# A two-block transformer kernel on one core: in the second block's skewed norms, ScalarE writes each shifted tile one weight unit later

## The chip, the cores and the metric

The kernel runs on one core of a Trainium2 chip. The metric is the device time of one execution in microseconds. Five things work side by side in a core: TensorE multiplies (PE in the profile; PEld is its loading of the stationary operand), VectorE (DVE), ScalarE (ACT), GpSimd (POOL), and SyncE (SP), which here only issues DMAs. Each engine takes its own instructions strictly in order; they meet through semaphores, on which an engine stops until another has counted far enough.

## The reference

The program is two transformer blocks in a row, each of two layers, on 256 tokens of width 1024. The first block mixes windowed attention, a short convolution and blocked attention, then a SwiGLU. The second block has two streams of 256 tokens, context and latent. A stream goes through an adaptive norm, a SwiGLU with a gated residual, a mixer (convolution, latent attention, Fourier mixing) and another SwiGLU, all modulated by vectors from a conditioning input. What matters here is the norm before each part:

```python
def rms_norm(x, g):
    xf = x.astype(jnp.float32)
    y = xf * lax.rsqrt(jnp.mean(xf * xf, axis=-1, keepdims=True) + EPS)
    return (y * g.astype(jnp.float32)).astype(x.dtype)

def ada_norm(h, g, shift, scale):
    return rms_norm(h, g) * (1 + scale) + shift

# in second_block, for each layer
h = h + HALF * gt1 * swiglu_2(ada_norm(h, g_ffn1[l], sh1, sc1), w1_ffn1[l], w3_ffn1[l], w2_ffn1[l])
u = ada_norm(h, g_mix[l], sh2, sc2)
```

## The kernel before

**Units.** All weights stream once through the core in 850 units. A unit is 128 output features by up to 8 blocks of 128 inputs, 512 KB. Each unit passes four steps. SP loads it into one of four slots (`raw`). ACT rounds it to the multiplier's precision (`high`, the CAST at L606, `whi<-raw`). DVE makes the remainder (`low`, L1141, `wlo<-raw,whi`). PE multiplies: three products per block (high by high, high by low, low by high; L2042 to L2044, or L1960 to L1962 where two units are interleaved), so 24 matmuls of 256 columns for one stream of 256 tokens. ACT and DVE work three units ahead (`AHEAD = 3`). `high` of unit u waits until PE has finished unit u-4, whose slot it takes.

**Tiles of the activations.** They lie with features on the partitions, in eight tiles (`m` = 0 to 7) of 128 by 512 columns: the context stream in columns 0 to 255, the latent stream in 256 to 511. They are split into a high and a low part too (`uhi`, `ulo`).

**The skewed norm.** The norm of one stream is hidden behind the matmuls of the other. While PE goes through a stage of units for the other stream, ACT squares the residual's tiles (L754), POOL adds the squares (L534), PE sums over features, ACT takes the root (L759), DVE inverts it, and PE spreads it over the partitions. Then each tile takes three steps:

- DVE scales it, `half_apply` (L1478, `big<-h,scl,aux`);
- ACT adds the shift and rounds, `half_shift` (L765, `uhi<-big,mod`);
- DVE makes the remainder, `half_low` (L1484, `ulo<-big,mod,uhi`).

The tables `DOWN`, `UP`, `INTO`, `INTO_LAST` and `AT_CHANGE` say after which unit j of the stage each tile is taken: one or two tiles per unit. In ACT's and DVE's programs a function `then(j)` is called at the end of step j of the stage. A step of ACT is: `high` of unit j+3, what else ACT does for unit j (a bank read out, the square of a tile), then `then(j)`. A step of DVE is: what it does for unit j (in the down stages the residual update, L1666), `low` of unit j+3, then `then(j)`, which scales the tiles of j and makes the remainders of the tiles of j-1. So DVE makes a remainder one unit after it scaled that tile.

**Where it is used.** Nine passes over a stage carry such a norm: the context part of the second block's first down projection (`fdown100c`), the second pass of four down or output projections (`fdown102`, `bout0`, `fdown202`, `fdown112c`; called a seam, with the table `DOWN`), and the first units of the stage behind each of those four (`mix0`, `fup200c`, `fup110c`, `mix1`). One more such norm, of the context stream beside the first block's last stages, is ordered by a function of its own that the diff leaves alone.

**What follows.** The stage for which a norm was made begins with two units interleaved (`two_units`, L1960): PE first waits for the `low` of both, and then, block by block, for one tile's remainder each.

## Time and profile before

| | |
|---|---|
| median of 3 runs | 3005.26 us (3005.05 to 3005.29) |
| span of the profiled execution | 3003.9 us |
| PE busy | 2897.1 us, 96% |
| DVE busy | 2051.9 us, 68% |
| ACT busy | 1366.5 us, 45% |
| POOL busy | 153.3 us, 5% |
| chain that ended last | PE 82%, DVE 9%, ACT 4%, issue 3%, DMA 2% |

The profiled execution has no device time of its own in the profile beside its span; the median of the unprofiled runs is 1.4 us longer than that span. PE's matmuls overlap: each lasts some 0.28 us while the next starts 0.11 us after it. So a share of 96% can still hide short stops, and where a row says that PE was idle for x us, the starts lie x + 0.28 us apart instead of 0.11, so that about 0.17 us more than x is lost. Line numbers are those of the kernel before.

### The profile page before, as it was taken

What the parts mean: (1) busy time and instruction counts of PE and PEld (TensorE: products, weight loads), DVE (VectorE), ACT (ScalarE), POOL (GpSimd) and SP (SyncE); (2) the same over time, 40 slices, a digit from 0 to 9 for tenths busy, and PEclk for the clock granted to TensorE, in tenths of its full rate; (3) what the DMA queues carried; (4) which work ended last, traced back from release to release, by engine and by line L of the source; (5) the groups of instructions that cost most, each with busy time, mean ns of one, the idle gap of its engine ahead of it and who ended that gap; (6) DMA issues with size and microseconds to landing.
All of it is one profiled execution on the core that took longest, in us unless ns stands there. A gap on an engine that the chain in (4) does not pass through costs nothing.

```text
span 3003.9 us, 59994 instructions
## 1 busy us (share of the span) xinstructions
PE 2897.1 (96%) x23648; PEld 2789.5 (93%) x23648; DVE 2051.9 (68%) x3323; ACT 1366.5 (45%) x2212; POOL 153.3 (5%) x222
## 2 busy tenths in 40 slices
PE   8999999999999999999999999999999999899998
PEld 8889999888999999998889999999999999779998
DVE  4658786658678777778764476867768566876655
ACT  5555445555446432354544354223542235545543
POOL 0000000000000000010000020000200001000000
PEclk9999999999999999999999999999999999999999
DMA  6435764435666565552212354544645445225454
GB/s 235 146 115 187 243 235 163 149 108 176 211 210 198 193 222 194 177 184 67 81 45 89 105 185 161 206 156 171 208 162 207 144 152 187 64 82 192 161 184 138
DMA packets 148053, 487.54 MB, mean 162 GB/s; under 512 B 16400, under 2 KB 25872, under 8 KB 147728
## 3 DMA queue, kind: packets, MB, share of 16 engines
q1 hardware_dynamic: 126688, 407.22, 41.0%
q0 software_dynamic: 21168, 77.60, 7.6%
q8 instruction: 135, 2.21, 0.3%
q14 instruction: 62, 0.51, 0.1%
HBM read 482.66 MB, written 1.05 MB: 161 GB/s over the span
## 4 chain that ended last, share of the span: by engine, by line
PE 82%; DVE 9%; ACT 4%; issue 3%; DMA 2%; POOL 0%; DVEq 0%; ACTq 0%; SPq 0%; POOLq 0%
PE bank L2042 23%; PE bank L2043 22%; PE bank L2044 22%; DVE wlo L1141 3%; ACT whi L606 2%; PE bank L1960 2%; PE bank L1961 2%; PE bank L1962 2%; DVE acc L1742 2%; PE aux L2269 1%; PE bank L2287 1%; DMA bbb<-in_w_ada 1%; PE bank L2120 1%; DMA raw<-in_w_stream 1%; DMA big<-in_w_ada 1%
## 5 line engine op out<-in xcount | busy, mean ns | idle before, releaser
L2042 PE MATMUL bank<-uhi,whi 128*128 128x256 f32 x4968 | 1397.0, 281 | 9.6 <-DVE wlo L1141 6.0
L2044 PE MATMUL bank<-uhi,wlo 128*128 128x256 f32 x4968 | 1381.1, 278 | 0.0
L2043 PE MATMUL bank<-ulo,whi 128*128 128x256 f32 x4968 | 1380.9, 278 | 0.0
L1141 DVE TENSOR_TENSOR wlo<-raw,whi 128x1024 fp32r<-128x1024 f32 (+4 forms) x850 | 951.0, 1121 | 370.7 <-ACT whi L606 362.2
L2042 PEld LDWEIGHTS bank<-uhi,whi 128*128 128x128 f32 x4968 | 935.1, 188 | 28.2 <-issue 22.9
L606 ACT CAST whi<-raw 128x1024 fp32r<-128x1024 f32 (+4 forms) x850 | 811.5, 961 | 282.7 <-PE bank L2044 179.3
L2043 PEld LDWEIGHTS bank<-ulo,whi 128*128 128x128 f32 x4968 | 934.8, 188 | 3.4 <-issue 3.0
L2044 PEld LDWEIGHTS bank<-uhi,wlo 128*128 128x128 f32 x4968 | 937.7, 189 | 0.0
L2042 PE MATMUL bank<-yhi,whi 128*128 128x256 f32 x1740 | 494.1, 284 | 16.2 <-DVE wlo L1141 8.5
L2043 PE MATMUL bank<-ylo,whi 128*128 128x256 f32 x1764 | 491.3, 279 | 0.0
L2044 PE MATMUL bank<-yhi,wlo 128*128 128x256 f32 x1740 | 484.5, 278 | 0.0
L2042 PEld LDWEIGHTS bank<-yhi,whi 128*128 128x128 f32 x1740 | 328.9, 189 | 25.4 <-issue 10.1
L2043 PEld LDWEIGHTS bank<-ylo,whi 128*128 128x128 f32 x1764 | 333.3, 189 | 3.2 <-issue 2.7
L2044 PEld LDWEIGHTS bank<-yhi,wlo 128*128 128x128 f32 x1740 | 329.8, 190 | 0.0
L706 ACT CAST yhi<-pp 128x256 fp32r<-128x256 f32 (+3 forms) x108 | 53.8, 498 | 320.7 <-DVE pp L1328 320.5
L1328 DVE TENSOR_TENSOR pp<-pp,bank 128x256 f32<-128x256 f32 (+1 forms) x108 | 57.6, 533 | 201.1 <-PE bank L2044 201.1
L1216 DVE CUSTOM_DVE_ANT_0 acc<-big,cs 128x1024 f32<-128x1024 f32 x128 | 156.3, 1221 | 24.8 <-DMA big<-in_w_ada 23.1
L1666 DVE SCALAR_TENSOR_TENSOR h<-bank,hgt,h 128x256 f32<-128x256 f32 x168 | 77.3, 480 | 108.9 <-PE bank L2044 75.7
L703 ACT ACTIVATE pp<-bank 128x256 f32<-128x256 f32 (+1 forms) x108 | 51.1, 473 | 174.7 <-PE bank L2044 173.6
L1216 DVE CUSTOM_DVE_ANT_0 acc<-vt,cs 128x1024 f32<-128x1024 f32 x102 | 124.6, 1222 | 2.2
L1960 PE MATMUL bank<-uhi,whi 128*128 128x256 f32 x240 | 73.0, 304 | 29.7 <-DVE ulo L1183 17.2
L1742 DVE SCALAR_TENSOR_TENSOR acc<-vpad,par,acc 128x512 f32<-128x512 f32 (+1 forms) x180 | 100.8, 614 | 0.0
(297 smaller groups left out, 2939.0 us busy)
## 6 DMA issues: line engine op xcount, KB each, us to landing
raw<-in_w_stream SPq DMA_DIRECT2D x674, 512.0 KB, 3.7
big<-in_w_ada POOLq DMA_DIRECT2D x64, 512.0 KB, 3.6
vt<-in_w_ada POOLq DMA_DIRECT2D x51, 512.0 KB, 3.7
raw<-in_w_stream SPq DMA_DIRECT2D x80, 256.0 KB, 2.7
raw<-in_w_stream SPq DMA_DIRECT2D x48, 384.0 KB, 3.1
bbb<-in_w_ada POOLq DMA_DIRECT2D x29, 512.0 KB, 4.7
raw<-in_w_stream SPq DMA_DIRECT2D x32, 192.0 KB, 2.4
raw<-in_w_stream SPq DMA_DIRECT2D x16, 128.0 KB, 2.0
```

The costliest lines, as they stand in the source:

```text
L606: sc.copy(whi[:, u % SLOTS, 0:n], raw[:, u % SLOTS, 0:n]).then_inc(s_high, 1)
L1141: ve.tensor_tensor(wlo[:, u % SLOTS, 0:n], raw[:, u % SLOTS, 0:n], whi[:, u % SLOTS, 0:n].bitcast(F32), ALU.subtract).then_inc(s_low, 1)
L1216: ve.tensor_tensor_reduce(out_, ring(name)[r], cs[:, s, :].rearrange("p (a b) -> p a b", a=out_.shape[1]), 1.0, 0.0, ALU.mult, ALU.add, su ...
L1328: ve.tensor_tensor(hid(k)[:, c0:c1], sg(k)[:, c0:c1], bank(u0, j)[:, c0:c1], ALU.mult).then_inc(read(u0, j), 1)
L1666: ins = ve.scalar_tensor_tensor(h[:, m, cols], bank(u0, j)[:, cols], gate(m, s), h[:, m, cols], ALU.mult, ALU.add)
L1742: ins = ve.scalar_tensor_tensor(a, v, wk, a, ALU.mult, ALU.add)
L1960: te.matmul(out_, whi[:, s, w], hi(k)[:, c0:c1], start=k == 0, stop=False)
L1961: te.matmul(out_, whi[:, s, w], lo(k)[:, c0:c1], start=False, stop=False)
L1962: ins = te.matmul(out_, wlo[:, s, w], hi(k)[:, c0:c1], start=False, stop=k == n - 1)
L2042: te.matmul(out_, whi[:, u % SLOTS, w], hi(k)[:, cols], start=k == 0, stop=False)
L2043: te.matmul(out_, whi[:, u % SLOTS, w], lo(k)[:, cols], start=False, stop=False)
L2044: ins = te.matmul(out_, wlo[:, u % SLOTS, w], hi(k)[:, cols], start=False, stop=k == plan.kt[u] - 1)
```

## The change

ACT's part of the skewed norms changes; nothing is added to or taken from any engine's work. `half_shift` of the tiles of unit j is now called in `then(j+1)`, so behind `high` of unit j+4 and behind what ACT does for unit j+1. When a step brings tile 7, the last, it is shifted in that same step, after those that still wait. The passes named above get it, the eight through `follow` and `fdown100c` directly.

```diff
+            def late_shifts(l, which, s, tiles):
+
+                waiting = []
+
+                def then(j):
+                    while waiting:
+                        half_shift(l, which, s, waiting.pop(0))
+                    waiting.extend(tiles.get(j, ()))
+                    while DT - 1 in waiting:
+                        half_shift(l, which, s, waiting.pop(0))
+                return then
+
...
-                    for m in f.tiles.get(j, ()):
-                        half_shift(l, which, s, m)
+                    shifts(j)
+                shifts = late_shifts(l, which, s, f.tiles)
                 return then
...
                     stream(U["fdown100c"], 8, 4, lambda j, i: None,
-                           then=lambda j: [half_shift(0, 0, 1, m) for m in AT_CHANGE[j]])
+                           then=late_shifts(0, 0, 1, AT_CHANGE))
```

On ACT, at the end of the seam `fdown102`, with `mix0` behind it. CAST is `high`, `big1<-h` the square of the other stream's tile, `uhi<-big1,mod` the shift. Before:

```order
L606 CAST whi<-raw 128x1024 [waits unit_used,unit_landed0]
L754 ACTIVATE big1<-h 128x256 [waits bank_read0]
L765 ACTIVATE uhi<-big1,mod 128x256 [waits half_applied] x2
L606 CAST whi<-raw 128x1024 [waits unit_used,unit_landed1]
L754 ACTIVATE big1<-h 128x256 [waits bank_read1]
L765 ACTIVATE uhi<-big1,mod 128x256 [waits half_applied]
L606 CAST whi<-raw 128x1024 [waits unit_used,unit_landed2]
L754 ACTIVATE big1<-h 128x256 [waits bank_read2]
L765 ACTIVATE uhi<-big1,mod 128x256 [waits half_applied]
```

And after:

```order
L606 CAST whi<-raw 128x1024 [waits unit_used,unit_landed0]
L754 ACTIVATE big1<-h 128x256 [waits bank_read0]
L765 ACTIVATE uhi<-big1,mod 128x256 [waits half_applied]
L606 CAST whi<-raw 128x1024 [waits unit_used,unit_landed1]
L754 ACTIVATE big1<-h 128x256 [waits bank_read1]
L765 ACTIVATE uhi<-big1,mod 128x256 [waits half_applied] x2
L606 CAST whi<-raw 128x1024 [waits unit_used,unit_landed2]
L754 ACTIVATE big1<-h 128x256 [waits bank_read2]
L765 ACTIVATE uhi<-big1,mod 128x256 [waits half_applied] x2
```

The first CAST here rounds unit 0 of `mix0`. The shift of tile 3 used to stand right before it and now stands behind it and its square; tiles 4 and 5 moved from before the second CAST to behind it, and tile 6 joined tile 7 in the last step.

On ACT, at the end of `fup200c`, whose up projections alternate between the two reads of a pair (`pp<-bank` the activation, `yhi<-pp` the rounding of the product). Before:

```order
L606 CAST whi<-raw 128x1024 [waits unit_used,unit_landed1]
L703 ACTIVATE pp<-bank2 128x256 [waits unit_used]
L765 ACTIVATE uhi<-big1,mod 128x256 [waits half_applied]
L606 CAST whi<-raw 128x1024 [waits unit_used,unit_landed2]
L706 CAST yhi<-pp 128x256 [waits bank_read3]
L765 ACTIVATE uhi<-big1,mod 128x256 [waits half_applied]
L697 ACT_TABLE_LOAD
```

And after:

```order
L606 CAST whi<-raw 128x1024 [waits unit_used,unit_landed1]
L703 ACTIVATE pp<-bank2 128x256 [waits unit_used]
L765 ACTIVATE uhi<-big1,mod 128x256 [waits half_applied]
L606 CAST whi<-raw 128x1024 [waits unit_used,unit_landed2]
L706 CAST yhi<-pp 128x256 [waits bank_read3]
L765 ACTIVATE uhi<-big1,mod 128x256 [waits half_applied] x2
L697 ACT_TABLE_LOAD
```

The rows look alike, but the single shift is that of tile 6 before and that of tile 5 after; the pair at the end is tiles 6 and 7. On PE, DVE, POOL and SP every instruction stands where it stood.

## Rows read from the trace of the kernel before

**Rows 1.** The page, part 1: busy time and share of each engine.
```profile
PE 2897.1 (96%) x23648; PEld 2789.5 (93%) x23648; DVE 2051.9 (68%) x3323; ACT 1366.5 (45%) x2212; POOL 153.3 (5%) x222
```

**Rows 2.** Waits, whole span: who waited for whom, us, times, longest.
```profile
DVE wlo L1141 <- ACT whi L606: 362.2, 256, 6.0
...
ACT uhi L765 <- DVE big L1478: 114.4, 68, 3.8
```

**Rows 3.** Timeline of PE, eight moments: start us, us, matmul [idle before <-releaser].
```profile
1002.01 0.36 PE L1960 MATMUL bank<-uhi,whi 128*128 128x256 f32 x1 [0.95 <-DVE wlo L1141]
...
1305.20 0.36 PE L1960 MATMUL bank<-uhi,whi 128*128 128x256 f32 x1 [1.20 <-DVE wlo L1141]
...
1777.48 0.35 PE L1960 MATMUL bank<-uhi,whi 128*128 128x256 f32 x1 [0.76 <-DVE wlo L1141]
...
1813.63 0.36 PE L1960 MATMUL bank<-uhi,whi 128*128 128x256 f32 x1 [2.24 <-DVE wlo L1141]
...
2144.68 0.36 PE L1960 MATMUL bank<-uhi,whi 128*128 128x256 f32 x1 [1.19 <-DVE wlo L1141]
...
2181.20 0.36 PE L1960 MATMUL bank<-uhi,whi 128*128 128x256 f32 x1 [1.59 <-DVE wlo L1141]
...
2512.75 0.36 PE L1960 MATMUL bank<-uhi,whi 128*128 128x256 f32 x1 [1.19 <-DVE wlo L1141]
...
2540.42 0.38 PE L1960 MATMUL bank<-uhi,whi 128*128 128x256 f32 x1 [0.41 <-DVE ulo L1484]
```

**Rows 4.** The chain that ended last, 1299 to 1305: start us, us, what.
```profile
1299.16 1.04 ACT whi L606
1300.21 0.02 issue
1300.23 1.23 DVE wlo L1141
1301.45 0.40 DVE big L1478
...
1301.88 0.41 ACT uhi L765
...
1302.30 0.49 ACT uhi L765
1302.79 0.95 ACT whi L606
...
1303.77 1.24 DVE wlo L1141
```

**Rows 5.** Timeline of DVE at the same place: start us, us, instruction.
```profile
1301.37 0.86 DVE L1478 SCALAR_TENSOR_TENSOR big<-h,scl,aux 128x256 f32<-128x256 f32 x2
1302.16 0.48 DVE L1484 SCALAR_TENSOR_TENSOR ulo<-big,mod,uhi 128x256 fp32r<-128x256 f32 x1
1302.55 0.48 DVE L1666 SCALAR_TENSOR_TENSOR h<-bank,hgt,h 128x256 f32<-128x256 f32 x1
```

**Rows 6.** Windows: busy us and counts by engine, granted clock, DMA share, GB/s.
```profile
1825.00:1845.00 20.00, 20.00 (x179) 20.00 (x178) 11.53 (x16) 9.54 (x15) 0.00 (x0) 1.00 0.63 206
2186.00:2206.00 20.00, 20.00 (x172) 20.00 (x171) 12.33 (x16) 12.27 (x18) 0.00 (x0) 1.00 0.61 203
1814.70:1818.10 3.40, 3.40 (x18) 3.40 (x18) 2.59 (x5) 1.67 (x4) 0.00 (x0) 0.50 0.55 182
```

**Rows 7.** Timeline of DVE, two moments in `fup100`, up to the next stage.
```profile
1022.14 1.23 DVE L1216 CUSTOM_DVE_ANT_0 acc<-big,cs 128x1024 f32<-128x1024 f32 x1 [4.11 <-DMA big<-in_w_ada]
...
1046.43 1.23 DVE L1216 CUSTOM_DVE_ANT_0 acc<-big,cs 128x1024 f32<-128x1024 f32 x1 [4.89 <-DMA big<-in_w_ada]
```

**Rows 8.** Timeline of POOL beside `fdown102` and `mix0`: sums of squares.
```profile
1288.28 0.73 POOL L534 TENSOR_TENSOR big<-big 128x256 f32<-128x256 f32 x1 [4.70 <-ACT big L754]
...
1304.19 1.39 POOL L534 TENSOR_TENSOR big<-big 128x256 f32<-128x256 f32 x1 [2.14 <-ACT big L754]
...
1311.44 2.71 POOL L534 TENSOR_TENSOR big<-big 128x256 f32<-128x256 f32 x1 [2.71 <-ACT big L754]
```

## The prediction

> **What bounds the kernel now.** I read the page's busy shares first. PE is busy for 2897.1 of 3003.9 us, and DVE for 68% [rows 1]. So the time is PE's work plus the places where PE stops, some 100 us in all, and a change on ACT can only take away stops or add them. The second view is the waits. DVE's `low` waited for ACT's rounding 256 times, 362.2 us in all; ACT's shift waited for DVE's scaling 68 times out of 80, 114.4 us [rows 2]. Each engine waits for the other. Neither sum is a loss by itself, since both work three units ahead of PE. The third view, PE's timeline, says where it becomes one: the first matmul of a new stage, where two interleaved units need both their `low` parts. PE stands idle there until `low` arrives, at 1002, 1305, 1777, 1813, 2144, 2181 and 2512 us, and at 2540 until a norm's remainder arrives [rows 3]. All eight are the ends of stages in which ACT and DVE carry a skewed norm.
>
> The chain of waits shows why. Just before the stop at 1305 it doesn't touch PE: rounding on ACT, `low` on DVE, scaling on DVE, two shifts on ACT, and the next rounding [rows 4]. In ACT's queue the shift stands ahead of the next rounding, and it waits for a scaling that stands in DVE's queue behind the `low` of the last rounding. So the two engines, which could work side by side, take turns. One turn with two tiles goes from 1299.16 to 1302.79, 3.6 us; with one shift (0.49) fewer it is 3.1. PE takes a unit in 2.72 us: 179 matmuls touched 20 us, of which about three only overlap its edge, so 0.113 us each, times 24 [rows 6]. With eight tiles in six units the turns are (4 x 3.1 + 2 x 3.6) / 6 = 3.3 us, so the lead over PE shrinks by some 0.6 us a unit until it is gone.
>
> **What the change does to a seam.** No instruction comes or goes, so its direct cost is zero; only the turns are broken. I replay DVE and ACT at `fdown102`, with start-to-start times from the rows: `low` 1.14, scaling, remainder and update 0.40 each (0.39 between the starts at 1302.16 and 1302.55 for an instruction of 0.48; 0.79 for the two scalings) [rows 5], rounding 0.95 and shift 0.41 [rows 4].
> - ACT: the next rounding now asks only that PE is done with unit j-1, and comes before the shifts. Its work per unit is 0.95 + 0.41 (the square, which has no row here and is priced as the shift) + up to 0.82 = 2.2 us, under 2.72.
> - DVE: six units with eight tiles are 6 x (0.40 + 1.14) + 8 x 0.79 = 15.6 us against 6 x 2.72 = 16.3 for PE. It keeps up, barely, and starts each unit's residual update when PE is done.
> - The second `low` of `mix0`, which started at 1303.77, then needs: PE done with `fdown102`'s unit 6 (the stage could have started at 1305.20 - 1.20 - 0.17 = 1303.83, and unit 7 takes 2.72, so at about 1301.1), 0.3 for the semaphore, the update, then 1.14: ready at about 1303.0. PE no longer stops.
> - What is late next is the last tile's remainder. PE ends unit 7 at about 1303.8; then 0.3, update 0.40, `low` 1.14, scaling and its end 0.5, shift 0.5, remainder 0.5: 3.3 us later. PE needs it for the eighth block, after 7 x 6 x 0.113 = 4.8 us. It has 1.4 us to spare, which is why tile 7 not being held back matters.
>
> The `mix` and `fup` stages with a norm go alike. In `fup` a pair of units costs DVE 2 x 1.14 for `low`, 0.8 for the product and its remainder, and 2 x 0.79 for tiles, 4.7 us against 5.44. A shift now stands behind ACT's read of the unit that PE just ended, so DVE may stand before a remainder until 0.3 + 0.4 + 0.5 = 1.2 us after that unit; the `low` behind it then ends 2.7 us after it and is needed 5.4 us after it at the earliest. That new wait is covered. In `mix1`, with two tiles a unit, the same sum gives 3.6 of 5.4.
>
> **The sum.** A stop costs its idle time plus 0.17 (matmuls of 0.28 start every 0.11). The eight stops are 0.95 + 1.20 + 0.76 + 2.24 + 1.19 + 1.59 + 1.19 + 0.41 = 9.53 us idle [rows 3], plus 8 x 0.17: 10.9 us. Behind the longest the granted clock is 0.50, 1.2 GHz, from 1814.7 to 1818.1: 18 matmuls touched it where 30 would have run [rows 6]; with that stop gone, half of 3.4 us, 1.7, comes back. The first stop gives more than it shows: behind it lies a stretch where DVE, not PE, is last, waiting for its own loads of the modulation weights (4.11 and 4.89 us), each issued after the product before it [rows 7]. All that moves with DVE. PE could start the stage at 1002.01 - 0.95 - 0.17 = 1000.9 [rows 3]. ACT's last shift, which frees its next rounding, would then begin 0.3 + 0.4 + 1.14 + 0.5 later, at 1003.2. Now it begins when the `low` of the stop has ended, at about 1001.8, and another scaling (0.4) and a turn (3.1) have passed: at 1005.3. So this chain gains 2.1 us, 1.0 beyond the stop; its bounds are 0 and 1.0, and I take 1.0, since no clock time anchors it. For smaller stops of the same kind, too short for rows, an estimate of 0.4, under the shortest in the rows. Sum 10.9 + 1.7 + 1.0 + 0.4 = 14.0 us. On the profiled span 3003.9 that is 2989.9; the median lies 1.4 above the span, so 2991.3.
>
> **What the trace can't price: the cadence of matmuls.** At granted clock 1.00 the same matmuls run at two rates: 179 touch 20 us in `fup200l`, 172 in `fup110l`, the same stage one layer on [rows 6]. That is 2.72 or 2.83 us a unit, 4%. The rate changes at stops and at matmuls of other shapes; how far each stretch reaches I read from such counts in many windows, of which these two are shown. Without the stops at 1777 and 2144, PE should keep the rate that it came with: slow into `fup200c` and on to about 1870, 93 us x 4% = 3.7 us lost; fast into `fup110c` to about 2238, 3.7 us gained. Nothing explains the rate, so I take zero net, with bounds of 8 us gained (the slow rate, which now runs from about 2777 nearly to the end, gone there: some 200 us x 4%) and 7 lost.
>
> **A rule against the change.** POOL's sums of squares run beside DVE: one alone takes 0.73 us, beside `low` 1.39, beside a long clearing of a buffer 2.71 [rows 8]; the `low` that it overlaps takes its usual 1.24 [rows 4]. So the sum pays, not DVE, and 1.4 per tile fits into 2.72. The Trainium skill, "SBUF — State Buffer", section "SBUF: two separate sides", says that a GpSimd operation and a DVE operation with two SBUF inputs take an exclusive lock, and the later one fully blocks. By that rule DVE would lose up to 1.4 us a unit where it now has 0.1, and a seam would be as late as today; the trace agrees for POOL, not for DVE.
>
> **Rivals.**
> - *Half stays.* DVE has only 0.7 us in 16 to spare in a seam. If its real pace is 5% worse, or if it is held up by POOL's 1.4 us beside a `low` [rows 8], the four seams' stops at 1305, 1777, 2144 and 2512 stay, 4.34 us idle and 4 x 0.17 [rows 3], 5.0 in all, and the time is 2996. For it: the thin margin. Against: the `low` that isn't longer beside POOL [rows 4]. The rule above would bring it about. Chance 0.13.
> - *No change.* ACT's order isn't what holds `low`, but the load of the weights or DVE itself, and the stops stay: 3005. Against: the chain names no DMA there [rows 4]. Also a later stage, last on DVE's convolution, could swallow what came before 1400, 5 us; but it starts from PE's progress and would move too. Chance 0.05.
> - *Slower, by the slow rate.* PE comes into `fup200c` at the slow rate; if nothing resets it through the fast stretches that follow (1778 to 2127 and 2249 to 2495, 595 us), 4% of them, 24 us, is lost against 14 gained: 3015. It decides from 350 us of lost fast rate on. Against: the slow rate in `fup110` ended at a stage with 512 columns at 2238, and `fdown200` has one at 1870. Chance 0.03.
>
> **How the numbers follow.** The forecast has 0.79. Its range is 2991.3 with 8 down and 7 up for the rate, some 2984 to 2998; the chain of loads moves it by 1 at most. It takes in the first rival; the other two, 0.08, and the tails of the rate are left out. A change under 0.2%, 6 us, can't be told from none here. Faster by more: the forecast's 0.79 less 0.02 for a bad rate, and 0.12 of the first rival, 0.89. Within: 0.01 of each of these two and the second rival's 0.05, 0.07. Slower: 0.01 for the rate and the third rival's 0.03, 0.04.
>
> **What would show it.** Of PE's eight stops, those behind `low` should be gone or under 0.2 us. ACT's waits for the scaling should fall from 114 us to under 30. The granted clock should stay at 1.00 around 1800 to 1820 and PE's first matmul of `mix0` should follow the last of the seam by 0.11 us. The new wait to look for is DVE's remainder behind ACT's shift, a few tenths each and off PE's path. I am wrong if PE waits for remainders instead (`ulo` L1484) or if its count in 20 us of `fup200l` falls to 172 and stays there.

## The result, and the profile after

The changed kernel takes 2984.59 us (median of 5 runs, 2981.64 to 2989.76), against 3005.26 before. The ratio is 0.9919, 95% interval 0.9893 to 0.9945: 20.7 us less by the medians, where 14.0 were forecast. The profiled execution has a span of 2983.8 us and a time of 2985.66.

The three runs that stood behind the time before lay within 0.24 us of each other; that was chance. Over all runs here, on several chips, the kernel before took 2989.7 to 3026.5 us (73 runs, mean 3005.7, standard deviation 8.2) and the changed one 2979.6 to 2999.0 (20 runs, mean 2986.2, deviation 4.8). The difference of the means is 19.5 us, give or take 2.8. One profile against one is therefore worth little for anything that differs by under 10 us, and most of what follows was read from several profiles of each kernel.

Busy time of the engines, from the page of after (for [rows 1]):

```profile
PE 2886.5 (97%) x23648; PEld 2780.8 (93%) x23648; DVE 2051.3 (69%) x3323; ACT 1369.5 (46%) x2212; POOL 143.3 (5%) x222
```

The counts of instructions are the same. The waits of after, in the columns of [rows 2]; its lines behind 767 have moved down by 12, so `low` is L1153 and the scaling L1490:

```profile
DVE wlo L1153 <- ACT whi L606: 340.8, 226, 6.2
ACT uhi L765 <- DVE big L1490: 53.4, 42, 4.2
```

ACT's wait for the scaling has halved from 114.4 us, not fallen under 30. It no longer matters, since what stands behind it has changed. PE's timeline at the places of [rows 3], the first matmul of two interleaved units (L1972); the first two rows are the end of the seam ahead of `mix0`:

```profile
1305.71 0.28 PE L2055 MATMUL bank<-ylo,whi 128*128 128x256 f32 x1
1305.83 0.28 PE L2056 MATMUL bank<-yhi,wlo 128*128 128x256 f32 x1
1305.94 0.28 PE L1972 MATMUL bank<-uhi,whi 128*128 128x256 f32 x1
...
1775.53 0.28 PE L1972 MATMUL bank<-uhi,whi 128*128 128x256 f32 x1
...
1809.19 0.28 PE L1972 MATMUL bank<-uhi,whi 128*128 128x256 f32 x1
...
2137.16 0.28 PE L1972 MATMUL bank<-uhi,whi 128*128 128x256 f32 x1
...
2170.81 0.28 PE L1972 MATMUL bank<-uhi,whi 128*128 128x256 f32 x1
...
2498.78 0.28 PE L1972 MATMUL bank<-uhi,whi 128*128 128x256 f32 x1
```

None has idle time before it, and each takes 0.28 us, not 0.36. `mix0` starts 0.11 us behind the last matmul of the seam, as foretold. The two stops without a row here, at `fup100` and on `mix1`'s remainder, are gone too.

Timeline of ACT, then of DVE, in the seam ahead of `mix0` in after (for [rows 4, 5]):

```profile
1299.06 0.41 ACT L754 ACTIVATE big<-h 128x256 f32<-128x256 f32 x1
1300.02 0.51 ACT L765 ACTIVATE uhi<-big,mod 128x256 fp32r<-128x256 f32 x1 [0.55 <-DVE big L1490]
1300.75 1.05 ACT L606 CAST whi<-raw 128x1024 fp32r<-128x1024 f32 x1 [0.22 <-PE bank L2056]
1301.71 0.41 ACT L754 ACTIVATE big<-h 128x256 f32<-128x256 f32 x1
1302.99 0.91 ACT L765 ACTIVATE uhi<-big,mod 128x256 fp32r<-128x256 f32 x2 [0.86 <-DVE big L1490]
1303.80 1.04 ACT L606 CAST whi<-raw 128x1024 fp32r<-128x1024 f32 x1
```

```profile
1300.96 0.47 DVE L1678 SCALAR_TENSOR_TENSOR h<-bank,hgt,h 128x256 f32<-128x256 f32 x1
1301.35 1.21 DVE L1153 TENSOR_TENSOR wlo<-raw,whi 128x1024 fp32r<-128x1024 f32 x1
1302.48 0.86 DVE L1490 SCALAR_TENSOR_TENSOR big<-h,scl,aux 128x256 f32<-128x256 f32 x2
1303.27 0.47 DVE L1496 SCALAR_TENSOR_TENSOR ulo<-big,mod,uhi 128x256 fp32r<-128x256 f32 x1
1303.67 0.47 DVE L1678 SCALAR_TENSOR_TENSOR h<-bank,hgt,h 128x256 f32<-128x256 f32 x1
1304.06 1.21 DVE L1153 TENSOR_TENSOR wlo<-raw,whi 128x1024 fp32r<-128x1024 f32 x1
```

The rounding at 1300.75 starts when PE has let go of the buffer. The one at 1303.80 starts right behind two shifts, about 0.3 us later than PE's progress would allow (PE began its next unit at 1303.22). But the weights that DVE's `low` needs at 1304.06 were rounded at 1300.75, ahead of those shifts. So ACT still waits at its shift, and what it delays isn't needed yet. DVE has no idle time in these rows: from `low` to `low` are 2.71 us, what PE takes for a unit.

Windows of after, columns as in [rows 6]:

```profile
1802.00:1812.00 10.00, 10.00 (x90) 10.00 (x90) 8.33 (x16) 5.48 (x11) 0.00 (x0) 1.00 0.56 195
1825.00:1845.00 20.00, 20.00 (x179) 20.00 (x178) 11.20 (x15) 10.47 (x15) 0.00 (x0) 1.00 0.57 189
2186.00:2206.00 20.00, 20.00 (x179) 20.00 (x178) 11.20 (x15) 9.84 (x15) 0.00 (x0) 1.00 0.58 188
```

In the first window, around the start of `fup200l` at 1809.19, the granted clock is 1.00, the level of 2.4 GHz; behind the same start it was 0.50 before. The third window has 179 matmuls where the same stage had 172.

Not everything improved. Timelines of DVE and of PE at the start of `fdown100` in after:

```profile
1055.51 1.22 DVE L1228 CUSTOM_DVE_ANT_0 acc<-big,cs 128x1024 f32<-128x1024 f32 x1 [2.45 <-DMA big<-in_w_ada]
...
1056.66 1.22 DVE L1153 TENSOR_TENSOR wlo<-raw,whi 128x1024 fp32r<-128x1024 f32 x1
```

```profile
1057.93 0.58 PE L2054 MATMUL bank<-yhi,whi 128*128 128x256 f32 x1 [2.22 <-DVE wlo L1153]
```

Here `low` stands in DVE's queue behind a product that waits for its load of modulation weights, and PE stops for 2.22 us. It is the chain of loads of [rows 7], one place later.

**An account over many profiles.** For each profile I took the distances between the starts of neighbouring 256-column matmuls: what lies over 0.13 us is a stop (less 0.113), what a distance between 0.10 and 0.13 has over 0.1133 is slow rate. Some 39 us of "elsewhere" are distances at matmuls of other shapes, about the same in all kernels. "Seams" here means the stages that wait for a skewed norm, `mix0`, `fup200c`, `fup200l`, `fup110c`, `fup110l` and `mix1`, and not the passes in which the norm is made; "loads" are `fup100`, `fdown100` and `fup101`.

| profile | span | stops: seams | loads | elsewhere | slow rate |
|---|---|---|---|---|---|
| before | 3003.9 | 39.7 | 6.9 | 149.1 | 35.2 |
| before_again1 | 2988.8 | 38.8 | 6.8 | 151.2 | 19.3 |
| before_again2 | 3002.8 | 37.9 | 8.3 | 154.3 | 29.6 |
| before_again3 | 2997.0 | 37.7 | 11.4 | 149.4 | 25.3 |
| before_again4 | 3008.1 | 37.4 | 6.4 | 151.6 | 38.4 |
| before_short_sums | 3010.5 | 37.2 | 9.7 | 155.0 | 35.7 |
| only_fdown100c | 2996.6 | 39.5 | 7.1 | 147.1 | 29.5 |
| after | 2983.8 | 26.3 | 4.0 | 156.5 | 23.0 |
| after_again | 2987.0 | 27.0 | 10.0 | 153.3 | 23.0 |
| after_again2 | 2993.2 | 26.9 | 5.8 | 150.5 | 36.3 |
| only_follow | 2984.2 | 27.6 | 11.5 | 141.8 | 30.2 |
| dve_first | 2974.3 | 28.0 | 2.7 | 151.1 | 19.4 |
| both | 2993.7 | 31.8 | 0.0 | 150.7 | 38.0 |
| both_short_sums | 2983.2 | 26.7 | 0.3 | 152.5 | 31.3 |
| dve_load | 3001.7 | 29.0 | 7.3 | 152.5 | 39.8 |
| pair_matmuls | 2988.8 | 26.8 | 0.3 | 155.5 | 33.1 |
| odd_matmuls | 3006.2 | 27.7 | 9.7 | 152.7 | 43.2 |
| reset512 | 3013.6 | 27.4 | 4.4 | 147.4 | 45.8 |

(`lone_same` has a span of 2973.5, 6.5 us of stops in the loads and 21.2 us of slow rate; the border behind its `mix1` can't be placed, so its other stops aren't split.) The seams' column is the change: 37 to 40 us with ACT's old order, 26 to 28 with the new one, in every profile but those in which DVE was given more or other work (`dve_first` 28.0 with ACT's old order, `both` 31.8, `dve_load` 29.0). The loads' column scatters from 6.4 to 11.5 us with ACT's old order in `fdown100c` (2.7 in `dve_first`), and from 0.0 to 10.0 with the new one.

### The profile page after: what moved, and what is told of

Read it like the earlier page. It is cut to its first block, busy times and chain, and to the rows that moved or that the text cites. A ratio compares the mean times of both kernels' runs of the same rounds, so it can differ in the third digit from the quotient of the medians.

```text
span 2983.8 us, 59994 instructions
## 1 busy us (share of the span) xinstructions
PE 2886.5 (97%) x23648; PEld 2780.8 (93%) x23648; DVE 2051.3 (69%) x3323; ACT 1369.5 (46%) x2212; POOL 143.3 (5%) x222
## 4 chain that ended last, share of the span: by engine, by line
PE 85%; DVE 7%; ACT 3%; issue 2%; DMA 2%; POOL 0%; DVEq 0%; SPq 0%; ACTq 0%; POOLq 0%
PE bank L2054 24%; PE bank L2056 23%; PE bank L2055 23%; PE bank L1972 2%; PE bank L1973 2%; PE bank L1974 2%; DVE acc L1754 2%; DVE wlo L1153 2%; ACT whi L606 1%; PE aux L2281 1%; DMA bbb<-in_w_ada 1%; PE bank L2299 1%; DMA raw<-in_w_stream 1%; PE bank L2132 1%; PE aux L2288 1%
## 5 line engine op out<-in xcount | busy, mean ns | idle before, releaser
L1153 DVE TENSOR_TENSOR wlo<-raw,whi 128x1024 fp32r<-128x1024 f32 (+4 forms) x850 | 950.4, 1120 | 349.2 <-ACT whi L606 340.8
L1972 PE MATMUL bank<-uhi,whi 128*128 128x256 f32 x240 | 71.2, 297 | 21.2 <-DVE ulo L1195 18.2
```

The lines of the kernel that those rows point to most:

```text
L1153: ve.tensor_tensor(wlo[:, u % SLOTS, 0:n], raw[:, u % SLOTS, 0:n], whi[:, u % SLOTS, 0:n].bitcast(F32), ALU.subtract).then_inc(s_low, 1)
L1972: te.matmul(out_, whi[:, s, w], hi(k)[:, c0:c1], start=k == 0, stop=False)
```

## Experiments

Ratios are to the kernel before, run beside on the same chip.

**The parts of the change.** `only_follow` delays the shifts in the seams and the `fup` stages alone, `only_fdown100c` only those of that stage. The two edits, each beside the new function:

```
-                    for m in f.tiles.get(j, ()):
-                        half_shift(l, which, s, m)
+                    shifts(j)
```

```
-                           then=lambda j: [half_shift(0, 0, 1, m) for m in AT_CHANGE[j]])
+                           then=late_shifts(0, 0, 1, AT_CHANGE))
```

`after_again` is the changed kernel once more.

> The eight passes that go through follow shift one unit later; fdown100c keeps the order of before. If the loss is the turns that ACT and DVE take, the stops at the starts of mix0, fup200c, fup200l, fup110c, fup110l, mix1 and inside mix1 are gone (9.8 us) and the half clock behind the longest with them, while the stop at the start of fup100 stays at 0.9 to 1.0 us of idle time, and that before fdown100. If it had been another thing that the new order changes, such as when weights land, the stop of fup100 would move too. Time by the first: 2988 to 2994, less or more by the rate of matmuls.

> The complement: only fdown100c shifts one unit later. Turns: the stop at the start of fup100 (0.95 us idle) is gone, ACT's last shift in that pass begins about 2.1 us earlier after PE's last unit of the pass, and the product with the modulation weights that waits for its load in fup100 starts that much earlier; the other seven stops and the half clock stay. Gain 2 us by the prediction's sum, 3 by the stops of the changed kernel's profile; 3002 to 3004 at an unchanged rate of matmuls. If the gain of this pass was only the stop itself, 1.1 us, the later wait for the load before fdown100 takes the rest back.

> The changed kernel, unaltered. Two theories of why it gained 20 us where 14 were forecast. If the two rates of matmuls (one each 0.113 or each 0.118 us) are drawn anew in each execution, the stops of PE are those of its first profile, within 1 us in sum over the passes that the change touches, but the time spent at the slower rate differs from the 756 us of the first profile by 50 us or more, and the span moves by 4% of that difference. If the rate is a fixed consequence of the new order, this profile shows the same stretches at the slower rate, again 750 to 760 us, and the times agree within 0.3 us.

Measured: `only_follow` 2987.32 us (8 runs), 0.9928 [0.9897, 0.9958]; `only_fdown100c` 3006.54 (10 runs), 0.9993 [0.9969, 1.0016]; `after_again` 2983.88 (6 runs), 0.9916 [0.9886, 0.9946]. PE's timeline at `fup100` in `only_follow`, and at `fup110l` in `only_fdown100c`:

```profile
996.60 0.36 PE L1972 MATMUL bank<-uhi,whi 128*128 128x256 f32 x1 [0.97 <-DVE wlo L1153]
```

```profile
2175.25 0.36 PE L1972 MATMUL bank<-uhi,whi 128*128 128x256 f32 x1 [2.91 <-DVE wlo L1153]
```

Each part takes away the stops of its own place and leaves the others, so the cause is local. The gain is that of `follow`. The late shifts of `fdown100c` remove the stop at `fup100`, but what they are worth is lost in the scatter of the loads: in `after_again` the same chain of loads stops PE for 3.80 us at 1059.89. `after_again` has the same 23.0 us of slow rate as the first profile, but in other stretches: 4.2 us of it in `fdown101` and `fup102`, where `after` has 0.2, and 0.2 in `fdown100` and `fup101`, where `after` has 3.4. So the stretches aren't a fixed consequence of the order.

**Another cure for the same turns.** `dve_first` keeps ACT's order of before; DVE scales its tiles ahead of `low`, so that ACT's shift, which still stands ahead of the rounding, finds them ready. `both` has this and the change. The added call stands ahead of `low`, and `first` issues the scalings:

```
+                        getattr(then, "first", nothing)(j)
...
-                def then(j):
+                def first(j):
```

> ACT's order of before, but DVE scales the tiles of unit j before it makes the low part for unit j+3, in all nine passes. This breaks the ring at its other end: ACT's shift no longer waits behind low. If the turns are the cause, all eight stops go as in the changed kernel, although ACT's rounding still stands behind the shift, and ACT's waits for the scaling fall from 114 us to less than 60. If what mattered is that ACT rounds the weights early, the stops stay, because the shift still stands ahead of the rounding. Time by the first theory as the changed kernel, 2980 to 2991; by the second 3000 to 3006.

> The changed ACT order together with DVE's scaling ahead of low. If one break of the ring is enough, this is the changed kernel again: no stop behind low at the eight places, 2980 to 2990. If ACT still lost time in waits for the scaling that mattered, the wait for scaling falls from 53 us to under 20 and the time falls by more than 2 us below the changed kernel's. A loss is possible where the last tile of a seam: the remainder is made after low as before, so its time stays.

Measured: `dve_first` 2986.25 us (10 runs), 0.9938 [0.9911, 0.9964]; `both` 2991.27 (6 runs), 0.9944 [0.9922, 0.9966]. The first gives the same gain, as far as these runs can tell, with ACT's queue untouched: it is the turns that cost, not the place of the shift as such. The second is no better than either, and its seams have 31.8 us of stops, which I had not expected. ACT's waits for the scaling are 62.9 us in `dve_first` and 32.3 in `both`, where I expected under 60 and under 20. Timelines of PE, of DVE and of POOL in `both`, ahead of `fup200c`:

```profile
1779.00 0.36 PE L1978 MATMUL bank<-uhi,whi 128*128 128x256 f32 x1 [0.96 <-DVE wlo L1153]
```

```profile
1774.77 1.71 DVE L1153 TENSOR_TENSOR wlo<-raw,whi 128x1024 fp32r<-128x1024 f32 x1
1776.40 0.47 DVE L1498 SCALAR_TENSOR_TENSOR ulo<-big,mod,uhi 128x256 fp32r<-128x256 f32 x1
1776.80 0.47 DVE L1685 SCALAR_TENSOR_TENSOR h<-bank,mod,h 128x256 f32<-128x256 f32 x1
1777.19 0.47 DVE L1492 SCALAR_TENSOR_TENSOR big<-h,scl,aux 128x256 f32<-128x256 f32 x1
1777.58 1.21 DVE L1153 TENSOR_TENSOR wlo<-raw,whi 128x1024 fp32r<-128x1024 f32 x1
1778.71 0.95 DVE L1498 SCALAR_TENSOR_TENSOR ulo<-big,mod,uhi 128x256 fp32r<-128x256 f32 x1
```

```profile
1774.65 0.74 POOL L534 TENSOR_TENSOR big<-big 128x256 f32<-128x256 f32 x1 [1.67 <-ACT big L754]
```

DVE is never idle, but the `low` at 1774.77, which began 0.12 us behind a POOL sum, takes 1.71 us, not 1.21, and some remainders take 0.95, not 0.47. The `low` of the last unit is late by that.

**Does POOL hold DVE?** `both_short_sums` and `before_short_sums` are `both` and the kernel before with this line ahead of POOL's sum; 224 of the 256 columns of each tile are left out of the sums of squares:

```
+                        cols = slice(s * S, s * S + 32)
```

> The kernel both, with POOL's sums of squares of the skewed norms taken over 32 of the 256 columns of each tile (224 columns are left out of the sums). In both, PE stops again at the first unit of mix0, fup200c, fup110c and mix1, 0.70, 1.12, 1.13 and about 1.1 us behind low, where the low starts 0.12 us after a POOL sum of 0.74 us and takes 1.71 instead of 1.22 us. Theory A (a DVE operation with two inputs in SBUF waits out a POOL sum that began before it): the low takes 1.2 us or at most 0.2 more, and the four stops shrink by 0.4 to 0.6 us each, to 0.1 to 0.7 us; the remainders that take 0.95 us fall to about 0.5. Theory B (the low is long for another reason, such as the transfers or ACT's work beside it, and the stops come only from the scalings that stand ahead of it): low and stops stay within 0.15 us of those in both.

> The kernel before, with POOL's sums of squares of the skewed norms over 32 of the 256 columns of each tile (224 are left out of the sums). Theory A (the stops of the kernel before come from the turns of ACT and DVE, not from POOL's hold on DVE): mix0, fup200c, fup200l, fup110c, fup110l and mix1 together keep 36 to 39 us of stops. Theory B (POOL's hold on DVE has a share in them, as it had in both, where shorter sums took the stops from 31.8 to 26.7): they fall by 3 us or more, to under 35.

Measured: `both_short_sums` 2985.03 us (one run; 2996.75 for the kernel before beside it), its seams' stops 26.7 where `both` has 31.8. Timelines of DVE, of POOL and of PE ahead of `fup200c`, for those of `both`:

```profile
1769.05 1.22 DVE L1154 TENSOR_TENSOR wlo<-raw,whi 128x1024 fp32r<-128x1024 f32 x1
1770.19 0.48 DVE L1499 SCALAR_TENSOR_TENSOR ulo<-big,mod,uhi 128x256 fp32r<-128x256 f32 x1
1770.70 0.48 DVE L1686 SCALAR_TENSOR_TENSOR h<-bank,mod,h 128x256 f32<-128x256 f32 x1
1771.10 0.47 DVE L1493 SCALAR_TENSOR_TENSOR big<-h,scl,aux 128x256 f32<-128x256 f32 x1
1771.49 1.22 DVE L1154 TENSOR_TENSOR wlo<-raw,whi 128x1024 fp32r<-128x1024 f32 x1
```

```profile
1772.26 0.56 POOL L535 TENSOR_TENSOR big<-big 128x32 f32<-128x32 f32 x1 [1.88 <-ACT big L755]
```

```profile
1773.32 0.28 PE L1979 MATMUL bank<-uhi,whi 128*128 128x256 f32 x1
```

`low` is back at 1.22 us, the remainders at 0.48, and all four stops are gone: more than the 0.4 to 0.6 us each that I expected. That the holds of several units add up in a seam where DVE has no idle time would explain it; I didn't replay it. `before_short_sums` took 3012.38 us (one run; 2995.23 beside it) and keeps 37.2 us of stops in the seams. Its PE at `mix0`:

```profile
1313.11 0.36 PE L1961 MATMUL bank<-uhi,whi 128*128 128x256 f32 x1 [1.20 <-DVE wlo L1142]
```

That is the 1.20 us of [rows 3]. The turns made the stops of the kernel before; a share of POOL's hold in them is too small for one profile to show (37.2 us, where the five profiles have 37.4 to 39.7).

**How thin DVE's margin is.** `dve_load` is the changed kernel with an instruction more in each seam unit from the third on:

```
+                    if j > 1:
+                        chained(ve.tensor_scalar(vpad[:, 0, 0, 0:S], cst0[:, 0:S], 1.0, None, ALU.mult))
```

> The changed kernel, with one more DVE instruction of 256 columns in each unit of a seam from its third on (some 0.3 to 0.4 us a unit; it writes to a buffer that nobody reads then). Theory A (the prediction's sum: DVE has 15.6 of 16.3 us for six units, so ACT's order helps only as long as DVE keeps up): DVE now needs some 17.7 us, the seams fall behind by about 1.4 us, and the four stops at the seams' ends (mix0, fup200c, fup110c, mix1) come back behind low with 0.5 to 1.5 us each, while fup200l and fup110l have none. Theory B (DVE has more to spare than the sum says): no stop above 0.3 us there. The rest as in the changed kernel.

Measured: 3003.60 us (one run, a slow draw of the rate, 39.8 us). PE at the start of `fup200c`, a timeline of `dve_load`:

```profile
1784.09 0.36 PE L1974 MATMUL bank<-uhi,whi 128*128 128x256 f32 x1 [0.26 <-DVE wlo L1153]
```

The stops return at three of the four places, but short (0.26 us idle, some 0.5 us in all against the changed kernel), and not at `mix0`; the added instruction took 0.32 us between starts. DVE's timeline, the added instructions and the `low` that PE waits for:

```profile
1771.74 0.53 DVE L1713 TENSOR_SCALAR vpad<-cst 128x256 f32<-128x256 f32 x1
...
1775.78 0.28 DVE L1713 TENSOR_SCALAR vpad<-cst 128x256 f32<-128x256 f32 x1
...
1778.91 0.28 DVE L1713 TENSOR_SCALAR vpad<-cst 128x256 f32<-128x256 f32 x1
...
1781.94 0.29 DVE L1713 TENSOR_SCALAR vpad<-cst 128x256 f32<-128x256 f32 x1
...
1782.66 1.22 DVE L1153 TENSOR_TENSOR wlo<-raw,whi 128x1024 fp32r<-128x1024 f32 x1
```

Only four of the six stand ahead of that `low`, 1.3 us, and they cost 0.5. So DVE has about 0.8 us to spare there, close to the 0.7 of the forecast's sum.

**The rate of the matmuls.** `odd_matmuls` is the changed kernel with one plain fp32 matmul ahead of `fup201` and one ahead of `fup202`; `pair_matmuls` has two at each place; `lone_same` has one of the usual kind (`whi` by `whi`, 256 columns). `reset512` has one of 512 columns ahead of each pair of interleaved 256-column units.

```
+                if (l, f) == (0, "2"):
+                    te.matmul(banks[7][:, 0:S], ones, cst0[:, 0:S], start=True, stop=True)
```

```
+                if c1 - c0 == S and n >= 4:
+                    te.matmul(banks[u % SLOTS][:, 0:T2], whi[:, u % SLOTS, 0:P], whi[:, u % SLOTS, 0:T2],
+                              start=True, stop=True)
```

> The changed kernel with two more matmuls on PE, of plain fp32 with 256 columns, whose results nobody reads: one ahead of fup201, one ahead of fup202, at 1906 and 2004 us in the changed kernel. Each takes some 0.45 us. If the rate of matmuls is a state that a matmul of another kind flips, as the spreading matmuls in the norms seem to do, the stretch between them, fup201 and fdown201, runs at the other rate than fup200 before and fup202 behind it: 90 us at 0.118 where the changed kernel's profile has 0.113, 3.8 us more, or the reverse. If the rate depends on the address or on the stage, nothing changes in these stages but 0.9 us for the two matmuls.

> The changed kernel with two plain fp32 matmuls of 256 columns ahead of fup201 and two ahead of fup202, where the kernel odd_matmuls had one each. Theory A (the rate hangs on whether an odd or an even number of such matmuls went before): both stages stay at the fast rate, excess 0.0 each. Theory B (any matmul of another shape there sets the slow rate): fup201 2.6 us and fup202 3.4 us of excess, as with one. Theory C (drawn anew each time): one of the two slow or none, and not the same again.

> The changed kernel with one matmul more of the usual kind (rounded weights, 256 columns) ahead of fup201 and of fup202. Theory A (the parity of the count decides): both go slow, 2.6 and 3.4 us of excess. Theory B (the other shape decides, its length or its format): both stay fast, 0.0.

> The changed kernel, with one matmul of 512 columns (its result is overwritten) ahead of each pair of interleaved units that has only 256 columns, so at the start of each stage of 256 columns. Theory A (the rate of 256-column matmuls is a state that a matmul of another shape may change, and a matmul of 512 columns leaves the fast one, as at fup110's end): the stretches at 172 matmuls in 20 us shrink to the first and last stages without such units, the excess over 0.113 us a matmul falls from 23 us (19 to 43 in the other profiles) to under 12, some 25 added matmuls cost 0.23 us each, 6 us, and the time is 2975 to 2982, ratio 0.990 to 0.992. Theory B (512 columns reset nothing; the rate is drawn anew at stops, or at any change of shape): the excess stays between 19 and 43 us with slow stretches that begin behind some of the added matmuls, and the time is 2985 to 3000. The touched stages' stops stay as in the changed kernel, 26 to 27 us without fup100 and fdown100, by both.

Measured: `odd_matmuls` 2992.82 us (7 runs), 0.9956 [0.9938, 0.9973]; `pair_matmuls` 2990.66 and `lone_same` 2975.30 (one run each); `reset512` 3005.95 (12 runs), 0.999 [0.9966, 1.0015]. One window inside `fup201`, 1930 to 1950, of `odd_matmuls`, of `pair_matmuls` and of `lone_same`:

```profile
1930.00:1950.00 20.00, 20.00 (x172) 20.00 (x171) 16.38 (x24) 6.23 (x8) 1.59 (x3) 1.00 0.62 214
```

```profile
1930.00:1950.00 20.00, 20.00 (x179) 20.00 (x178) 15.13 (x24) 5.50 (x8) 2.12 (x4) 1.00 0.56 191
```

```profile
1930.00:1950.00 20.00, 20.00 (x179) 20.00 (x178) 15.37 (x24) 6.01 (x8) 2.11 (x4) 1.00 0.50 159
```

This stage and `fup202` were at the fast rate in every profile but that of `odd_matmuls`. One odd matmul made both slow (2.6 and 3.4 us of excess), two left them fast, one of the usual kind left them fast. So the rate is a state, an instruction of another shape can change it, and a second one changed it back or prevented it. My idea that 512 columns reset it to fast is wrong: in `reset512`, `fdown202c` and `fdown112` turned slow with the added matmul at their start (0.86 us of excess each); the second is fast in all other profiles, the first in all but that of `odd_matmuls`. The kernel lost all that the change had gained, 28 x 0.23 = 6.4 us of it by the added matmuls themselves. Each variant of the single matmuls was profiled once. What the state is stays open.

**The same kernels again.** `before_again1` to `4` and `after_again2` are unaltered.

> The kernel before, unaltered, profiled once more. If the rate of matmuls is drawn anew at stops, its stretches at the slower rate lie elsewhere than in the first profile (848 us of slower time by the sum of excess over 0.1133 us per matmul). If the ring of ACT and DVE sets the pace where the norms are, the stops at fup200l and fup110l are near 1.8 us when PE comes in at the slower rate and 2.4 us or more, with a half clock behind, when it comes in at the faster one: a slower PE is not paid there, since the ring is slower than PE at either rate. If the ring is not what sets the pace, the stops are the same at both rates.

> As before_again1, a second draw, so that the sum of the stops in the touched passes (46.7 us in the first profile, 46.6 where only fdown100c was changed) has a spread: 44 to 52 us if the first profile was an ordinary one, 50 or more on average if the 22 us between the medians of all runs (3006.8 and 2984) come from stops that the first profile happened to have fewer of.

> The kernel before, unaltered, a fourth profile. If the runs' means tell of an excess that three profiles missed (61 runs of it have a mean near 3006, its three profiled executions 2998.5 us of span), its span lies near 3004 and the excess sits in the slow rate (over 30 us) or in stops outside the touched stages (over 152 us); the touched stages without fup100 and fdown100 have 38 to 40 us of stops whatever the rest does.

> The kernel before, unaltered, a fifth profile, with the same expectation: touched stages without fup100 and fdown100 38 to 40 us of stops; the rate and the other stops scatter.

> The changed kernel unaltered, once more, to see how far its time is from the kernel before in a second session and how much its profile differs from the two others. If the change is worth 12 us of stops plus a mean difference of matmul rates and loads near zero, the ratio is 0.994 to 0.997; if the two first measurements (0.9919 and 0.9916) hold, the median lies 22 to 25 us under the kernel before, more than the stops account for. In its profile the eight stops stay away, the touched stages without fup100 and fdown100 have 26 to 27 us of stops, and the excess of the slow rate is 19 to 43 us.

Measured: 2990.56, 3004.63, 2998.79 and 3009.93 us for the kernel before, one run each; `after_again2` 2987.46 (9 runs), 0.9945 [0.9920, 0.9970]. The five profiles of the kernel before have a mean span of 3000.1. Five of the changed one (three unaltered, `pair_matmuls` and `lone_same`, whose added matmuls cost under 2 us) have 2985.3. That is 14.9 us, with a standard error of 4.7; the difference of the means of all runs, 19.5, lies within it. One expectation of `before_again1` came true in the five profiles of the kernel before: the stop at the start of `fup110l` is 1.8 to 1.9 us where PE comes in at the slow rate (three of the five) and 2.5 to 2.6 where it comes in at the fast one. ACT's and DVE's turns set the pace there, not PE's rate.

## Why the prediction was half right

In short: the mechanism and its main term, the stops, were right. The step that failed is the cadence, "so I take zero net", and the bounds drawn from it. The profiles show 2.3 us less of the slow rate, 1.3 of it at the two places named, and a spread between executions of the same kernel (8.2 us standard deviation) for which the range had no term. The 2.3 us are themselves smaller than the scatter of single profiles, and where the rest of the gain beyond the forecast comes from stays open.

**The turns, right.** The forecast's reason was that ACT and DVE took turns. Three results carry it: each part of the change removes its own stops, another cure (`dve_first`) removes them with ACT's order as it was, and shorter POOL sums don't. By place, mean of five profiles before against four after (`lone_same` left out), with the forecast in brackets: `mix0` 1.9 us (1.4), `fup200c` 1.4 (0.9), `fup200l` 2.7 (4.1), `fup110c` 1.4 (1.4), `fup110l` 2.1 (1.8), `mix1` 2.0 (1.9). The sum is 11.5 us, from 38.3 to 26.8, and the forecast's terms for these places come to 11.5.

**The half clock, right by luck.** The 1.7 us were in `fup200l`'s term. Of the five profiles of the kernel before, only the first shows that slow clock there. The mean stop of `fup200l`, the lost clock included, is 2.7 us, so the clock's term should have been about 0.3. The other places were taken at or below what they gave, by up to 0.5 us, and that made up for it.

**The chain of loads, right in the mean and useless in one profile.** Forecast 2.1 us (the stop at `fup100` and 1.0 beyond). Loads' column: 8.0 before, 5.3 over five profiles after, 2.6 us less. But single profiles lie between 0.3 and 10.0 with the new order. Taking one chain's bounds as "0 and 1.0" was far too sure. The 0.4 us for smaller stops of the same kind show nowhere: the stops elsewhere rose.

**The cadence, the step that failed.** "Nothing explains the rate, so I take zero net." At the two places that the prediction named the reasoning was sound: without a stop PE keeps the rate it came with. Window at the same stage, `fup110l`, in `before_again3`, which fell to the slow rate behind its stop, for the window of after above:

```profile
2185.00:2205.00 20.00, 20.00 (x172) 20.00 (x171) 12.06 (x17) 12.09 (x17) 0.00 (x0) 1.00 0.62 205
```

With the stops there, `fup110` was slow in 3 of the 5 profiles of the kernel before; without them it was fast in all 5 after, as was the stage that PE came from. `fup200` took over the rate of `bout0`, slow in 2 of 5. In the mean `fup110` gained 1.9 us, where 3.7 were given for one profile, and `fup200` lost 0.6, not 3.7: about 1.3 us net, not zero. The first profile had been read as the kernel, when it was one draw. The slow rate as a whole went from 29.6 to 27.3 us, with a scatter of some 7 us from profile to profile: not clear of it, and too little to make up the rest.

**What stays open.** The profiles give 15 us, of which 11.5 in the seams, 2.6 in the loads and 2.3 in the rate, while stops elsewhere rose by 1 to 3 us. The runs give 19.5. The five or so between are within what ten profiles can tell, so I can't say whether the profiled executions of the kernel before were faster than its average one (mean time 3001.8, against 3005.7 over all its runs) or something is gained that they don't show. The measured median lies at the edge of the range, and by the ratio (0.9919 of 3005.26 is 2980.9) beyond it. The range's down side was 8 us for the rate of one stretch, with nothing for the difference between executions, which three runs within 0.24 us seemed to exclude.

**The waits.** ACT's wait for the scaling was to fall under 30 us; it is 53.4. It was the wrong witness: ACT waits there as before, with nothing urgent behind it. The new wait, DVE's remainder behind ACT's shift, is there as foretold: 4.7 us in 15 places, the longest 1.0, where it was 1.3 in 5.

**The rivals.** *Half stays* didn't happen. Its ground, DVE's thin margin, was real (0.8 us by `dve_load`, 0.7 in the forecast), but DVE kept the pace of the sum. `dve_load` and `both` show what it takes to bring stops back. *No change* and *slower* are refuted by the three ratios of the changed kernel (0.9919, 0.9916, 0.9945).

**The rule on POOL and DVE, misread.** The prediction said that POOL pays and DVE doesn't. It had looked at a `low` that began before the sum. Timeline of the kernel before, 1.1 us behind the start of the sum at 1304.19 in [rows 8], which ends at 1305.58; the row joins two remainders:

```profile
1305.30 0.96 DVE L1484 SCALAR_TENSOR_TENSOR ulo<-big,mod,uhi 128x256 fp32r<-128x256 f32 x2
```

The first of them began inside the sum and took 0.56 us, ending 0.28 behind it; alone it takes 0.48. In the kernel before, the changed one and `both` the later one waits: POOL's sum behind a `low` (1.39 where 0.73 is usual), a `low` behind a sum (1.71 where 1.21 is usual), a remainder behind a sum (0.56 in the kernel before, 0.73 in the changed one, 0.95 in `both`). The scaling, one of whose inputs is in PSUM, takes 0.47 inside a sum as outside. The Trainium skill, "SBUF — State Buffer", section "SBUF: two separate sides", says that whichever starts first has the shared ports for its whole instruction, and that a DVE operation with two SBUF inputs is one that can be held. By that rule the trace agrees, in both directions, but for the end: remainders that began 0.28, 0.45 and 0.67 us ahead of the end of a sum were held 0.08, 0.25 and 0.47 us, so they were let go about 0.20 us before POOL's record ends. The forecast's number still held since in the changed kernel DVE's `low` comes ahead of the scalings, and in the four seam passes of its first profile no `low` begins inside a sum (eight remainders do, held 0.25 us each).

## What to carry to other kernels

Where two engines feed each other through queues, look in the chain for waits that cross back and forth without touching the bottleneck engine; moving one instruction behind the next unit's urgent one, on either engine, breaks the turns, but doing it on both can fill the next engine up. Before a few tenths of a per cent are forecast, run the unaltered kernel often enough to know how it varies, and read the terms from more than one profile. When two engines share a port, look at pairs that overlap in both orders before saying who pays.

## What the runs showed of the hardware

- At a granted clock of 1.00 the 256-column matmuls have two rates, 0.113 and 0.118 us, and stay in one for up to hundreds of microseconds. It can change behind a stop and at a matmul of another shape (one plain fp32 matmul, or one of 512 columns, made the next stages slow; two of the first kind, or one of the usual kind, didn't). From 19 to 46 us of a profile go to the slow rate.
- The same program varies by 8.2 us (standard deviation, 73 runs over several chips; 8.8 in the 27 runs side by side on one). The mean granted clock of a run, 0.985 to 0.991, goes with a part of it: over 61 runs of the kernel before its correlation with the time is -0.44, which is a fifth of the variance.
- Between POOL's sum of squares and a DVE operation with two SBUF inputs the later one waits: the sum takes 1.39 us where 0.73 is usual, `low` 1.71 where 1.21 is, a remainder up to 0.95 where 0.48 is. A DVE operation with one input in PSUM keeps its 0.47 us. DVE is let go 0.14 (`low`) to 0.20 us (remainder) before the end of POOL's record.
- A POOL sum of 32 columns takes 0.25 us where no `low` holds it, one of 256 columns 0.74. The 0.56 us of the row shown above is a sum that began inside the `low` of 1771.49 and ended 0.11 us behind it. The first record isn't always the first served: the sum of 2.71 us at 1311.44 [rows 8] waited for two DVE operations, the clearing and a `low` that began 1.74 us before its end and took 1.16, and held only the next `low`. The remainders that begin inside a short sum begin in its last 0.20 us and take their usual 0.48. Timeline of POOL in `both_short_sums`:

```profile
1779.66 0.25 POOL L535 TENSOR_TENSOR big<-big 128x32 f32<-128x32 f32 x1 [6.83 <-ACT big L755]
```
